# Two layers of a hybrid decoder: how layer 0's recurrence gets its operands, and what runs beside it

## What is computed

```
for layer in range(DEPTH):                        # x: 1024 tokens x 1024, float32
    h = rms_norm(x, norm_mix_g[layer])
    if layer % 2 == 0:
        z = h @ even_w_in[j]
        aq, ak, av, iq, ik, iw, bq, bf, bi, bg = split_cols(z, EVEN_SPLITS)
        ...
        o_a = dsa_attention(aq, ak, av, iq, ik, iw)      # 256 best keys of each query, by an index score
        o_b = rms_norm(hgrn2(bq, bf, bi, lb_all[j]), b_out_norm_g[j]).reshape(b, s, MIX_HALF)
        o_b = o_b * silu(bg)
        mix = concatenate([o_a, o_b], axis=-1) @ even_w_out[j]
    else:
        ...                                              # conv and gated recurrence, window attention
    x = x + mix
    h = rms_norm(x, norm_mlp_g[layer])
    x = x + square(relu(h @ mlp_w_up[layer])) @ mlp_w_down[layer]

def hgrn2(q, f_logit, i, lb):                     # 4 heads of 128
    qf = silu(q); f = lb + (1 - lb) * sigmoid(f_logit); kf = 1 - f; bt = cumsum(log(f))
    # in a chunk: att[t, s] = sum_d qf[t, d] kf[s, d] exp(bt[t, d] - bt[s, d]) for s <= t
    # o = att @ v + (qf * exp(bt)) @ state
    # state = exp(b_last) * state + (kf * exp(b_last - bt))^T @ v
```

## Time and profile before

| what | value |
|---|---|
| median of 3 runs | 2771.32 us (2768.27 to 2773.56) |
| the profiled execution | 2770.24 us, span 2768.5 us |
| mean granted clock of TensorE | 0.943 |
| TensorE, VectorE, ScalarE, GpSimd busy | 91%, 59%, 37%, 50% of the span |
| start of the recurrence, 699 to 722 us | clock 0.50, 319 GB/s |
| body of the recurrence, 722 to 871 us | clock 0.85, GpSimd busy 147.5 us |
| output projection of layer 0, 881 to 989 us | clock 0.94, TensorE busy 97.3 us |

### The profile page before, as it was taken

How to read it: one execution, slowest core, us unless ns; L and a number is a source line. 1 busy time by engine, 2 the same in 40 slices (tenths; PEclk the granted TensorE clock), 3 DMA queues, 4 the chain that set the end, 5 groups by cost and what they waited for, 6 DMA issues and landing times.

```text
span 2768.5 us, 31272 instructions
## 1 busy us (share of the span) xinstructions
PE 2516.9 (91%) x11111; PEld 1997.3 (72%) x11133; DVE 1621.8 (59%) x2341; ACT 1017.0 (37%) x1704; POOL 1375.6 (50%) x767
## 2 busy tenths in 40 slices
PE   6888698789377989999999998998998999999999
PEld 4666586455376868888888887775766888888887
DVE  6578577984586334555444855657534455554483
ACT  4144477555353232323222233525344223322220
POOL 4312353566795045666555914316423566655591
PEclk8999799799788999999999999997989999999999
DMA  4211122000401022211112113102002221111211
GB/s 145 50 27 27 31 61 91 16 8 4 126 11 62 1 61 61 61 61 42 41 38 61 61 69 88 38 31 88 8 16 61 61 61 53 39 49 40 61 56 66
DMA packets 164290, 140.76 MB, mean 51 GB/s; under 512 B 23001, under 2 KB 137762, under 8 KB 163938
## 3 DMA queue, kind: packets, MB, share of 16 engines
q1 hardware_dynamic: 143058, 116.19, 14.0%
q10 hardware_dynamic: 21136, 23.34, 2.8%
HBM read 116.17 MB, written 13.63 MB: 47 GB/s over the span
## 4 chain that ended last, share of the span: by engine, by line
PE 67%; DVE 11%; issue 10%; POOL 6%; ACT 4%; ACTq 1%; DMA 0%; DVEq 0%; another core or an unknown queue 0%; POOLq 0%
PE ps L2085 20%; PE ps L2086 20%; PE ps L2087 20%; POOL cl L851 2%; POOL cl L849 2%; ACT signs L1175 2%; PE ps L2274 1%; PE ps L2191 1%; DVE ub L1978 1%; PE ps L2282 1%; DVE QL L1730 1%; DVE ps L1664 1%; PE ps L2262 1%; DVE o_den L1783 1%; POOL w_lo L694 1%
## 5 line engine op out<-in xcount | busy, mean ns | idle before, releaser
L2085 PE MATMUL ps<-h_hi,w_hi 128*128 128x512 f32 x1680 | 673.5, 401 | 13.6 <-POOL w_lo L712 9.7
L2086 PE MATMUL ps<-h_lo,w_hi 128*128 128x512 f32 x1680 | 662.5, 394 | 0.0
L2087 PE MATMUL ps<-h_hi,w_lo 128*128 128x512 f32 x1680 | 661.8, 394 | 0.0
L2085 PEld LDWEIGHTS ps<-h_hi,w_hi 128*128 128x128 f32 x1680 | 321.5, 191 | 83.6 <-issue 14.4
L2086 PEld LDWEIGHTS ps<-h_lo,w_hi 128*128 128x128 f32 x1680 | 321.1, 191 | 68.4 <-issue 3.9
L2087 PEld LDWEIGHTS ps<-h_hi,w_lo 128*128 128x128 f32 x1680 | 320.5, 191 | 68.5
L1975 DVE TENSOR_TENSOR x_res<-ps,x_res 128x1024 f32<-128x1024 f32 x224 | 268.7, 1220 | 115.3 <-PE ps L2087 115.3
L1956 DVE TENSOR_TENSOR u_all<-ps,u_all 128x512 f32<-128x512 f32 x112 | 77.3, 690 | 417.2 <-ACT u_all L1082 417.2
L712 POOL TENSOR_TENSOR w_lo<-w_raw,w_hi 128x1024 fp32r<-128x1024 f32 x112 | 266.9, 2400 | 103.7 <-ACT w_hi L1071 103.7
L2085 PE MATMUL ps<-w_hi,uo_hi 128*128 128x512 f32 x784 | 307.4, 392 | 3.1 <-DVE shared L1975 3.1
L2087 PE MATMUL ps<-w_hi,uo_lo 128*128 128x512 f32 x784 | 305.6, 390 | 0.0
(11 more groups left out here) (348 smaller groups left out, 4504.2 us busy)
## 6 DMA issues: line engine op xcount, KB each, us to landing
w_raw<-in_mlp_w_up SPq DMA_DIRECT2D x64, 512.0 KB, 4.0
w_raw<-in_mlp_w_down SPq DMA_DIRECT2D x64, 512.0 KB, 3.8
w_raw<-in_even_w_in SPq DMA_DIRECT2D x23, 512.0 KB, 3.7
w_raw<-in_odd_w_in SPq DMA_DIRECT2D x10, 512.0 KB, 3.7
x_res<-in_x SPq DMA_DIRECT2D x8, 512.0 KB, 8.1
x_res<-in_x ACTq DMA_DIRECT2D x8, 512.0 KB, 7.2
scr_x<-x_res SPq DMA_DIRECT2D x8, 512.0 KB, 2.6
x_res<-scr_x SPq DMA_DIRECT2D x8, 512.0 KB, 4.5
```

The lines of the kernel that those rows point to most:

```text
L2085: t_.matmul(out_, ah, bh, start=first, stop=False)
L2086: t_.matmul(out_, ah, bl, start=False, stop=False)
L2087: return t_.matmul(out_, al, bh, start=False, stop=last)
```

## The change

In layer 0: (a) `kf` and `qf` are kept by chunk, [chunk, 4 heads x 128], at a fixed distance from each other, so that one view takes keys for the first blocks and queries for the second, and GpSimd makes a level's product with one instruction of 512 columns. `bT` lies where the index queries were. The copies `bh` and `qh` are gone. (b) Values and gates come from DRAM by chunk, 16 transfers of 256 KB, into the free upper halves of `o_sum` and `o_den`, and `x` is loaded right behind them, at the start of the recurrence. (c) The output projection's attention half, 16 sums of four units, goes in the recurrence: after slots 0 and 2 of chunks 2 to 7 and after four slots behind the last chunk, all in bank 4, each added to `x` three slots later by VectorE. What remains behind the recurrence are 16 sums of the other four units, in banks 0 to 3, with the norm turned in banks 4 to 7. (d) ScalarE rounds the weights of units 4 to 26 of layer 0's input, of the last four of its output, and of units 4 to 17 of layer 1's input; what GpSimd still rounds it does with `tensor_scalar`. (e) The level masks are built in the attention, the diagonals of maxima by four instructions with a column as scalar, and three VectorE instructions at the end of the search are gone.

```diff
-        kf = at("kf", R_U + 16 * KB, [P, 4, S])
+        KQ = (M2 - M1) // 4
+        kq = at("kq", M1, [P, 2 * (KQ + HD)])
+        kf, qf = (kq[:, o:o + T * 512].rearrange("p (c f) -> p c f", c=T) for o in (0, KQ))
-        bT = at("bT", M1, [P, 4, S])
-        qf = at("qf", M2, [P, 4, S])
+        bT = at("bT", R_U + 16 * KB, [P, 4, S])
...
+        OA_SLOTS = [7 * c + l for c in range(2, T) for l in (0, 2)] + [7 * T + l for l in (0, 2, 4, 5)]
+        OA_LAG = 3
...
-                g.tensor_tensor(w_hi[:, k, :], w_raw[:, n % 2, :], ones, ALU.mult).then_inc(w_hi_ready, 1)
+                g.tensor_scalar(w_hi[:, k, :], w_raw[:, n % 2, :], 1.0, None, ALU.mult).then_inc(w_hi_ready, 1)
...
             for n in range(U_OUT0 + 4):
-                split_unit(n)
+                if 4 <= n < U_OUT0:
+                    split_low(n)
+                else:
+                    split_unit(n)
...
-                    g.tensor_tensor(by_head(diag[:, u % 3, :]), ident[:].unsqueeze(1).to_broadcast((P, 4, P)),
-                                    m.unsqueeze(2).to_broadcast((P, 4, P)), ALU.mult).then_inc(att["diag_ready"], 1)
+                    for h in range(4):
+                        ins = g.tensor_scalar(diag[:, u % 3, h * P:(h + 1) * P], ident[:], m[:, h:h + 1], None, ALU.mult)
+                    ins.then_inc(att["diag_ready"], 1)
...
                 for n in range(STEPS[layer]):
+                    if layer == 0 and n % 4 == 2 and n // 4 < 7:
+                        level_mask(n // 4)
...
-                e = cl[:, n % RING, :].rearrange("p (h b j) -> p h b j", h=4, j=2 * B)
-                keys = kf[:, :, tk].rearrange("p h (b j) -> p h b j", j=2 * B)
-                queries = qh[:, :, tk].rearrange("p h (b j) -> p h b j", j=2 * B)
+                e = cl[:, n % RING, :].rearrange("p (m s j) -> p m s j", s=2, j=B)
+                pairs = kq[:, 0:2 * (KQ + B)].rearrange("p (s r) -> p s r", s=2)[:, :, c * 512:(c + 1) * 512]
+                mixed = pairs.rearrange("p s (m j) -> p m s j", j=2 * B)[:, :, :, 0:B]
                 pool.wait_ge(hg["exp"], 2 * n + 2)
-                g.tensor_tensor(e[:, :, :, 0:B], e[:, :, :, 0:B], keys[:, :, :, 0:B], ALU.mult) \
-                    .then_inc(hg["prod"], 1)
-                g.tensor_tensor(e[:, :, :, B:2 * B], e[:, :, :, B:2 * B], queries[:, :, :, B:2 * B], ALU.mult) \
-                    .then_inc(hg["prod"], 1)
+                g.tensor_tensor(e, e, mixed, ALU.mult).then_inc(hg["prod"], 1)
...
-                if l == L_SPLIT:
...
+                if l == L_SPLIT and c >= 2 and c % 2:
+                    split_low(U_OUT0 + 4 + c // 2 - 1)
+            split_low(U_OUT0 + 7)
...
+            def round_weights(n):
+                if n in (4, U_MIX1 + 4):
+                    act.wait_ge(w_ready, n)
+                act.wait_ge(raw_landed[n % 2], landed[n])
+                for used in last_uses(n):
+                    act.wait_ge(*used)
+                s.activation(w_hi[:, slot_of(n), :], w_raw[:, n % 2, :], ACT.Copy).then_inc(w_hi_ready, 1)
...
-                act.dma_start(bh[:, :, tk], bT[:, :, tk]).then_inc(chunk_landed(c)[0], 16)
-                act.dma_start(qh[:, :, tk], qf[:, :, tk]).then_inc(chunk_landed(c)[0], 16)
-                if c == 1:
-                    act.dma_start(vB[:], scr_v).then_inc(vb_landed, 16)
-                    act.dma_start(sbg[:], scr_g).then_inc(sg_landed, 16)
+                act.dma_start(chunk_values(o_sum, c), heads(scr_v[:, c, :])).then_inc(chunk_landed(c)[0], 16)
+                act.dma_start(chunk_values(o_den, c), scr_g[:, :, c * P:(c + 1) * P]).then_inc(chunk_landed(c)[0], 16)
+            for t in range(T):
+                act.dma_start(x[:, t, :], a["x"][0, t * P:(t + 1) * P, :]).then_inc(x_landed[t], 16)
...
-            link(v.tensor_copy(score[:, 0:P], cbias[:, P:2 * P]))
-            link(v.memset(score[:, P:2 * P], 0.0))
-            link(v.tensor_copy(score[:, 2 * P:3 * P], cbias[:, P:2 * P]))
...
+                if n - OA_LAG in OA_SLOTS:
+                    i = OA_SLOTS.index(n - OA_LAG)
+                    dve.wait_ge(x_landed[i // 2], 32)
+                    dve.wait_ge(down_done, G_OUT0 + i + 1)
+                    part = x[:, i // 2, i % 2 * HT:(i % 2 + 1) * HT]
+                    v.tensor_tensor(part, ps[:, 4, :], part, ALU.add).then_inc(x_added, 1)
...
+                if n in OA_SLOTS:
+                    i = OA_SLOTS.index(n)
+                    ts_, cs = slice(i // 2 * P, (i // 2 + 1) * P), slice(i % 2 * HT, (i % 2 + 1) * HT)
+                    if i == 0:
+                        pe.wait_ge(w_ready, U_OUT0 + 4)
+                    pe.wait_ge(x_added, G_OUT0 + i)
+                    pe.wait_ge(hg["klT"], min(c, T))
+                    for k in range(4):
+                        ins = products(ps[:, 4, :], (h_hi[:, k, ts_], h_lo[:, k, ts_]),
+                                       (w_hi[:, k, cs], w_lo[:, k, cs]), k == 0, k == 3)
+                    ins.then_inc(down_done, 1)
-            pe.wait_ge(hg["o_lo"], T)
-            out_projection(1, U_OUT0, G_OUT0)
+            out_projection_of_recurrence(1, U_OUT0, G_OUT0 + 16)
```

More of the change, by code:

```diff
@@ L1322, in _ @@
                     act.wait_ge(hg["o_full"], d + 1)
-                    s.activation(h_hi[:, 4:8, d * P:(d + 1) * P], heads(vB[:, d, :]), ACT.Copy).then_inc(hg["o_hi"], 1)
-            act.wait_ge(hg["o_lo"], T)
-            for t in range(T):
-                act.dma_start(x[:, t, :], a["x"][0, t * P:(t + 1) * P, :]).then_inc(x_landed[t], 16)
+                    s.activation(h_hi[:, 4:8, d * P:(d + 1) * P], chunk_values(o_den, d), ACT.Copy).then_inc(hg["o_hi"], 1)
+                if l == L_SPLIT and c >= 2 and c % 2 == 0:
+                    round_last(c // 2 - 1 if c < T else 3)
             norm(1)
@@ L2179, in down_last @@
                         pe.wait_ge(u_ready, u1 + 8)
-                    down((u_hi, u_lo), [slot_of(n1 + 4 + j) for j in range(4)], g1 + 2 * t, 0, t)
+                    down((u_hi, u_lo), [slot_of(n1 + 4 + j) for j in range(4)], g1 + 2 * t, t)
                     if turns is not None and t >= 2:
@@ L2439, in _ @@
                             pe.wait_ge(hg["klT"], c)
+                        added = sum(m < n for m in OA_SLOTS)
+                        if added:
+                            pe.wait_ge(x_added, G_OUT0 + added)
                         for h in range(4):
```

187 lines of the change are left out of this document (103 added, 84 removed).

## The result

The changed kernel takes 2737.35 us (median of 4 runs, 2732.16 to 2740.61), the kernel before, measured beside it, 2770.31 (median of 4): a ratio of 0.9879, 95% interval 0.9864 to 0.9894. That is 33 us less, where 49 were forecast; the time lies where the rival "the body gets longer" put it (2731 to 2745), though the body grew by at least twice what that rival gave it.

The account below looks back on a forecast made before the run. TensorE, busy 91% of the span, was taken as the bound, idle or slow-clocked mainly in the recurrence. Terms -43 + 5 + 0 - 6 + 1 - 3 - 2 - 1 = -49 took 2770.2 to 2721 us, range 2700 to 2744.

Parts of the forecast that it names:

- the body gets longer: Rival: sums delay output products and the longer GpSimd instruction holds VectorE; chunk 20.5 to 21 us, 2731 to 2745 us; chance 0.27.
- The out-projection: Behind layer 0's recurrence: sums of 24 products become sums of 12, as in layer 1; -43 us (-45 to -39).
- The tail: End of the recurrence: four sums in bank 4 wait for additions, second half starts later; +5 us (+3 to +10).
- The body: Recurrence's eight chunks: GpSimd, VectorE and TensorE all come out near the present 18.6 us a chunk; 0 us (-17 to +14).
- The turn-taking with VectorE: Recurrence body: GpSimd's products and VectorE's subtractions exclude each other; as the only bound, about 17 us shorter, the lower end.
- The rival of the dear product: Rival, slower than before: GpSimd's product over keys and queries costs much more; 2795 us at 2.6 us each; chance 0.04.
- the shorter body: Rival: turn-taking was all that bound the recurrence body, which falls by 17 us; 2704 us, 2700 with a good start; chance 0.15.
- the last rival: Rival: moving the sums does nothing, since TensorE is full and 44 us come back in the body; 2760 us; chance 0.04.
- The start: Start of the recurrence: ScalarE's 24 DMA issues take 15 to 17 us, first exponential near 716; -6 us (-9 to +3).
- Masks and diagonals: Layer 0's attention: masks and four-instruction diagonals mostly covered by GpSimd's waits for exponentials; +1 us (-2 to +7).
- ScalarE's rounding and the end of the search: Layer 0's input and search: rounding moved off GpSimd, -3 us (-10 to +6); three instructions removed, -2 us (-2.6 to 0).
- Layer 1: Layer 1's projection: 14 weight roundings move to ScalarE, with no known wait for them; -1 us (-4 to +3).

Follow-up runs that it names:

- run 3: Changed kernel with additions five places behind their sums instead of three, and each attention diagonal built in one instruction again: 2726.9 us, body 164.1 us.
- run 8: Changed kernel with additions five levels behind their sums and each addition cut to 8 of 512 columns (result differs): 2717.3 us, body 161.7 us.
- Run 9: Run 6's kernel with each sum's twelve products issued as six behind one level and six behind the next: 2710.0 us, body 167.0 us.
- run 10: Run 6's kernel with the turn of a chunk's output, gate, high and low part one level later: 2715.1 us, body 170.8 us.
- run 6: Changed kernel with additions five levels behind their sums and loads of values, gates and x issued between the exponentials: 2709.6 us, 0.9778 of the kernel before.
- run 2: Changed kernel with GpSimd's level product in two halves of 256 columns and layer 0's input weights rounded by GpSimd again: 2747.7 us, body 181.0 us.
- run 11: Run 6's kernel with two sums in each of the eight chunks, none in the tail, and GpSimd's product in halves: 2706.7 us, 0.9778 of the kernel before.
- run 4: Changed kernel with loads of values, gates and x issued between the exponentials instead of ahead of the first: 2723.5 us, start 2.2 us.
- Run 5: Kernel before with only GpSimd's weight rounding and query-scale spreading turned into one-input multiplications by constant 1.0: 2763.7 us, threshold ready at 474.1 us.
- run 1: Changed kernel with all 16 sums behind the last chunk and level masks built behind the attention again: 2747.2 us, body 147.0 us, attention 218.2 us.

## Why the prediction was right in its range and 16 us off in its sum

**The out-projection** (-43, measured -44.9) and the price of a sum by it were right, from layer 1's stage. **The tail** was counted instruction by instruction and came out at +6.1 for +5.

**The body** is the step that failed: "all three engines so come out near the present 18.6", 0 us, measured +27.8. The two parts were both wrong in size. The turn-taking with VectorE was not worth the 17 us put at the lower end: without sums the body is 147.0 us, 1.4 below the kernel before, for VectorE's own 137 us then fill it. And the sums cost 29.2 us. I had compared each engine's work, 18.8 us for VectorE and 18.9 for TensorE with the sums, with the 18.6 us of a chunk. A chunk with sums then took 23.1 to 24.9 us from first exponential to first exponential, and the engines were not full in it: this stage of four engines in a circle was not paced by the fullest one. Waits at the head of an in-order queue were missing from the count. I had named the queue behind bank 4, as TensorE's wait for VectorE; the costly wait was the other way round, VectorE's for TensorE, because an addition three places behind its sum meets VectorE's own lead of three places. It accounts for 12.1 us (run 3). Where the other 17.1 us lie is open. VectorE's time for the additions is 2.4 of them (run 8). Run 9 took 10 us off ScalarE's waits for output products and turned keys, run 10 took 8 us off TensorE's at the turn; each time another wait grew, and the body was no shorter (167.0 and 170.8 us, 167.3 in run 6). VectorE is 90% busy in run 3. TensorE's waits for bank 4 (4.4 us) were never taken away, and no run kept everything but TensorE's sums.

The Trainium skill (SBUF — State Buffer, section Who interferes with whom) has a VectorE instruction with two SBUF inputs contend with a GpSimd instruction that reads SBUF. The trace agrees (`ek`'s argument 1.75 us beside the long products, 1.21 beside halves). What it costs is another matter: halves made the body 4.8 us longer with VectorE 80% busy (run 2) and 1.8 us shorter at 89% (run 11), and in both GpSimd had 12 to 16 us more work, so the price of the stretching alone is not shown.

**The rival of the dear product** is out: 1.46 us in the median, far from 2.2. So is the shorter body. The 5 us that the prediction estimated beside its sum, for the far-apart elements of level 0, did not come: that level's eight products took 1.42 us at the least and the others 1.26, a difference of 0.16 us each and not 0.6. **The longer body** as a rival named the right stage and got the total by luck: it gave a chunk 20.5 to 21 us and the body 10 to 14 more, and the body got 27.8; the search's unforeseen gain made up for the rest. (By its own 44 us the last rival's time is 2765, not 2760.)

**The start** (-6, measured -4.5) had its mechanism right, an ordered queue of issues ahead of the first exponential. One issue of 2.01 us and `x`'s eight in 5.38 instead of 3.96 made it longer. What I did not draw from the same rows is that the whole 18 us could go (run 4).

**Masks and diagonals** (+1, measured +5.0): the size was in the range, but half of the cause wasn't named, and what was named stood in the wrong place. The first low part of `P` starts 11.3 us after the threshold before and 17.7 after the change. (Behind it the rest of the stage took 1.4 us less.) The diagonals are 3.1 of these 6.4 us (14.6 with the old ones, run 3): the first of them are waited for, and are not in the idle time that the prediction put them in. GpSimd splits the last two weights of the stage as soon as TensorE has left the input products: from 473.05 to 481.7 before, all ahead of the threshold at 482.5; from 460.55 to 472.4 now, with the threshold at 463.6. So they fall into the preparation of the attention, where VectorE's copy of `ident` takes 2.26 us instead of 0.23. Run 5, with the old attention and splits that end 4.2 us after its threshold, lies between: 13.1 us. That fits, but no run moved the splits alone. Part of what the search won was handed back at once; the attention's end, 13.9 us earlier, holds both. What the masks add is small (run 1).

**ScalarE's rounding and the end of the search** (-3 and -2, measured -18.9): the term for the rounding, as run 2 and the changed kernel divide it, was 4.5 us less 1.2, so the size was near. Missing from the list altogether was the new form of GpSimd's rounding and spreading, a line of the diff that I read as neutral: 8.4 us by itself (run 5). By the pieces of run 5 the 18.9 us are 2.3, 4.9, 7.0 and 4.7. The first of them may be real: with a clock of 0.80 in the first 50 us four executions with the change took 236.0 to 236.8 us, and two without ScalarE's rounding, before and run 5, 238.5 and 239.7. No run shows what gives it.

**Layer 1** (-1, measured -1.7) can't be judged: the stage took 1786.6 to 1790.2 us in the kernels with the changed code, 1790.3 in the kernel before and 1789.7 in run 5.

The sum thus held by two misses that partly cancel: +27.8 in the body, unforeseen, and -13.9 up to the end of the attention, where -4 was forecast.

## What to carry to other kernels

When work is put into another engine's idle time, look not only at how idle the engines are but at where the reader of its result stands in the reading engine's queue: more places behind than that engine runs ahead. Here the lead is three places; five were worth 12 us over three, and other numbers were not tried. One number did it, and the profile names it in one line, the wait of the leading engine. And loads that are needed later don't belong ahead of the first instruction on the engine that issues them: 24 issues cost 18 us in front of the loop and 0 to 3 us in it (runs 4 and 6).

## What was not expected of the hardware

GpSimd's multiplication by a constant takes 2.77 us for 128 x 1024, its multiplication by ones from SBUF 1.89 us, and the threshold of the search is nonetheless ready 8.4 us earlier with the longer one (run 5).

The time to the last score differs by up to 5 us between kernels that have the same instructions up to there (232.7 to 237.8 us), with a granted clock of 1.00 or 0.80 in the first 50 us. The attention with the same code took 218.6 to 224.7 us. With differences of this size a stage can only be judged from a landmark right before it, and with its clock beside it.
